# The second layer's modulation dot products move from the first model's stages into a merge stage

## The chip, the cores and the metric

One core of one Trainium2 chip runs the whole program in one launch. The metric is the device time of that launch in microseconds. TensorE (PE) multiplies matrices, VectorE (DVE) and ScalarE (ACT) work on vectors, SyncE (SP) issues the DMAs that bring data from HBM into on-chip memory. Each engine has its own instruction stream; they meet by semaphores.

## The reference

Two models run one after the other on one sequence of 256 tokens of width 1024, in float32. The first has two layers of attention and a mixture of experts. The second has two layers, and each of its layers is modulated by six vectors that depend on a condition `c` alone, not on the tokens:

```python
def decoder_layer(x, c, ..., w_ada, b_ada, ...):
    mod = jax.nn.silu(c.astype(F32)) @ w_ada + b_ada        # (1, 6 * 1024)
    shift1, scale1, gate1, shift2, scale2, gate2 = jnp.split(mod, 6, axis=-1)
    h = modulate(rms_norm_2(x, norm1_g), shift1, scale1)
    ...
    gates = jax.nn.sigmoid((h @ w_gate + b_gate).astype(F32))
    merged = jnp.zeros(x.shape, F32)
    for i, y in enumerate((y_ret, y_rwkv, y_conv)):
        merged = merged + gates[..., i * d:(i + 1) * d] * (y @ w_branch[i])
    x = x + gate1[:, None, :] * (merged @ w_o)
    h2 = modulate(rms_norm_2(x, norm2_g), shift2, scale2)
    ...
```

`w_ada` has 1024 x 6144 numbers a layer, 24 MB of float32. The product with the single row silu(c) is what is called the modulation's dot products here. `y_ret`, `y_rwkv` and `y_conv` come from `h` through retention, RWKV and a short convolution; behind the last line stand the experts, weighted with gate2.

## The kernel before

All weights stream from HBM in chunks of 2 MB (128 partitions x 4096 float32) through `ring`, six slots. `load(sp, n, ...)` puts chunk n into slot n % 6; from chunk 6 on SyncE first waits until TensorE has counted `w_used` up to n - 5, so chunk n is issued when chunk n - 6 has been used. SyncE works through its list in order: what stands behind a waiting load waits too.

The stages are blocks, one after another, and a block ends when all engines have ended their part. In the first model a layer has `project1` (the input projection, four chunks), `latents`, `turn_qk`, `attention`, `head_rms_out` (the output projection, two chunks) and `moe` (the experts). In the second model a layer has `project2` (chunks 0 to 10), several stages of retention and RWKV, then `merge` (chunks 11 to 19), `project_out2` (20, 21) and `moe` (from 22).

The modulation's dot products run on VectorE. A chunk of `w_ada` holds four blocks of 1024 columns; for each, one instruction multiplies it by silu(c) (`c_all`, the same row on all partitions) and accumulates the sum over the columns into one column of `mod_sums`. `ada_load` brings chunk i of a stage into one of two places of the `arena`; from the third on it waits for `ada_used`, that is, for the dots of chunk i - 2. `ada_dots` waits for its chunk and does its four dots. A layer of the second model needs 12 chunks, 48 dots. Before the change the first model's layer l does those of the second model's layer l: 8 chunks in `project1` (`ADA1`), placed three, three and two ahead of VectorE's copies of the projection out of PSUM, and 4 in `head_rms_out` (`ADA2`), ahead of the residual additions of j = 0, 1, 3 and 5. `project2` of the second model reads `mod_sums` at its start.

`merge` has 24 steps m = 8 i + d (branch i, output block d). TensorE computes the gate product (8 matmuls from `xnT`) and the branch product (4 matmuls) of a step into the two halves of bank m % 8; ScalarE applies the sigmoid; VectorE multiplies both (L1402, L1404), counts `taken`, and from step 8 on adds the result to `merged` (L1406). From step 8 on TensorE waits for `taken` of step m - 8. Each branch uses three ring chunks: one to its step 3 (gate), one to its step 7 (gate), one to the branch product of its step 7. Here chunk 17 to 25 are loaded: `for n in range(MERGE + RING, OUT2 + RING)`.

A matmul of float32 shows as two records in the trace, so a gate product is 16 records and a branch product 8.

Of the kernel before, what the change touches and what calls it, by code (L numbers as in the profile page):

```python
# [19 lines left out]
ALU = mybir.AluOpType  # L20
# [4 lines left out]
L = 2  # L25
# [85 lines left out]
SMALL1 = 2 * UQ_N + UKV_N + KT * R1_N  # L111
SMALL2 = 2 * MW + KT * R2_N
CONV, RWKV, LORA, RET, MERGE, OUT2, MOE2 = 0, 3, 6, 7, 11, 20, 22
ADA1, ADA2 = 8, 4
MOE1 = 6


def build(nc, dram, out):
    ctx = ExitStack()
    with ctx:  # L120
# [106 lines left out]
        def ada_sems():  # L227
            return [sem(f"ada_in{i}") for i in range(2)], sem("ada_used")

        def ada_load(sp, sems, l, i, places):  # L230

            ada_in, ada_used = sems
            if i >= 2:
                sp.wait_ge(ada_used, i - 1)
            sp.dma_start(ar(places[i % 2], SLOT), dram["w_ada2"][l, i]).then_inc(ada_in[i % 2], 16)

        def ada_dots(dve, sems, l, i, places):

            ada_in, ada_used = sems
            dve.wait_ge(ada_in[i % 2], 16 * (i // 2 + 1))  # L240
            for j in range(4):
                w = ar(places[i % 2] + D * j, D)
                last = nc.vector.scalar_tensor_tensor(w, w, 1.0, c_all, ALU.mult, ALU.mult,  # L243
                                                      accum_out=mod_sums[:, l, 4 * i + j:4 * i + j + 1])
            last.then_inc(ada_used, 1)

        def setup():
            in_loaded, x_loaded, c_loaded = sem("in_loaded"), sem("x_loaded"), sem("c_loaded")
# [137 lines left out]
        def project1(l, ada):  # L386
            scaled = sem("n1a_scaled")
            places = (4096, 8192)
            with nc.Block() as block:
                @block.sync  # L390
                def _(sp):
                    for i in range(ADA1):
                        ada_load(sp, ada, l, i, places)
                    if l == 0:
                        for n in range(4, 6):
                            load(sp, n, *first_chunks(1, 0)[n])
                    for n in range(MOE1, MOE1 + 4):
                        load(sp, n, moe1_chunk(l, n))
# [35 lines left out]
                @block.vector  # L434
                def _(dve):
                    dve.wait_ge(sets[turn[0]]["vec_in"], 48)
                    norm_scale(dve, scaled, V1("attn_norm"), xnT)
                    for b in (1, 3, 5, 7):
                        if b < 7:
                            for i in ((0, 1, 2), (3, 4, 5), (6, 7))[b // 2]:  # L440
                                ada_dots(dve, ada, l, i, places)
                        dve.wait_ge(w_used(), b // 2 + 1)
                        nc.vector.tensor_copy(dests[b], bank[b][:, 0:REST if b == 7 else 512])

# [257 lines left out]
        def head_rms_out(l, ada):  # L702
# [8 lines left out]
            with nc.Block() as block:  # L711
                @block.sync
                def _(sp):
                    for i in range(ADA1, ADA1 + ADA2):
                        ada_load(sp, ada, l, i, places)
                    for n in range(MOE1 + 4, MOE1 + 6):
                        load(sp, n, moe1_chunk(l, n))

# [31 lines left out]
                def _(dve):  # L750
# [6 lines left out]
                    for n in range(4, 6):  # L757
                        for i in range(4):
                            j = 4 * (n - 4) + i
                            if j in (0, 1, 3, 5):  # L760
                                ada_dots(dve, ada, l, ADA1 + (0, 1, 3, 5).index(j), places)
                            if i < 3:
                                dve.wait_ge(proj_ready, 3 * (n - 4) + i + 1)
                            else:
                                dve.wait_ge(w_used(), n + 1)
                            nc.vector.tensor_tensor(hT[:, j, :], hT[:, j, :], out_bank(j)[:, 0:T], ALU.add).then_inc(norms[0], 1)
# [581 lines left out]
        def merge(l):  # L1348

            pair_ready, gate_ready, taken, s_dve = sem("mrg_pair"), sem("mrg_gate"), sem("mrg_taken"), sem("mrg_dve")  # L1350
            ys = (y_ret, y_rwkv, y_conv)
            sg = ar(13824, 4, T)
            tmp = ar(0, 2, T)
            with nc.Block() as block:
                @block.sync
                def _(sp):
                    for n in range(MERGE + RING, OUT2 + RING):
                        load2(sp, l, n)

                @block.tensor  # L1360
                def _(pe):
# [19 lines left out]

                @block.scalar
                def _(act):
                    for i in range(3):
                        for d in range(KT):
                            m = KT * i + d
                            if d < KT - 1:
                                act.wait_ge(pair_ready, (KT - 1) * i + d + 1)
                            else:
                                act.wait_ge(w_used(), MERGE + 3 * i + 3)  # L1390
                            if m >= 4:
                                act.wait_ge(taken, m - 3)
                            nc.scalar.activation(sg[:, m % 4, :], bank[m % 8][:, 0:T], ACT.Sigmoid, bias=V2("b_gate_2")[:, m:m + 1]).then_inc(gate_ready, 1)

                @block.vector
                def _(dve):
                    then = step(dve, s_dve)
                    for m in range(3 * KT):
                        d = m % KT
                        dve.wait_ge(gate_ready, m + 1)  # L1400
                        if m < KT:
                            nc.vector.tensor_tensor(merged[:, d, :], sg[:, m % 4, :], bank[m % 8][:, T:2 * T], ALU.mult).then_inc(taken, 1)  # L1402
# [592 lines left out]
```

## Time and profile before

| | us |
|---|---|
| median of 3 timed runs | 2921.86 (2912.44 to 2928.99) |
| the profiled execution | 2913.63 |
| its span from first to last instruction | 2911.7 |
| TensorE busy | 2280.5 (78%) |
| VectorE busy | 737.8 (25%) |
| ScalarE busy | 369.1 (13%) |
| DMA | 778.84 MB, mean 267 GB/s |

The span is the time between the first and the last instruction of the profiled execution; the device time is some 2 us more. Busy shares are means over stages with different limits: the expert stages move 400 GB/s and more, other stages hardly any data. A row of the timeline has the start, the length, the engine, the line, the operation, output and inputs, the count, and in brackets how long the engine stood idle before it and what released it. "issue", "PEq" and the like stand for waits at the border of blocks.

### The profile page before, as it was taken

How to read it: one execution, taken by the hardware profiler on the slowest of the kernel's cores; microseconds unless marked ns; L12 is line 12 of the kernel's file. 1: busy time of each engine (PE TensorE's matmuls, PEld its weight loads, DVE VectorE, ACT ScalarE, POOL GpSimd, SP SyncE). 2: the span in 40 equal slices, each digit the busy share in tenths (PEclk: the TensorE clock that was granted, in tenths of full speed). 3: DMA queues.
4: the chain of work that ended last, by engine and by line, in shares of the span. 5: the costliest groups of instructions: out<-in, count | busy, mean ns of one | idle time of the engine just before them, and what ended most of it. 6: DMA issues, size and time to landing. Idle time of an engine off the chain costs nothing. (4 is left out here: it accounts for less than half of the span.)

```text
span 2911.7 us, 30995 instructions
## 1 busy us (share of the span) xinstructions
PE 2280.5 (78%) x12840; PEld 1430.8 (49%) x12841; DVE 737.8 (25%) x1659; ACT 369.1 (13%) x732; POOL 5.2 (0%) x16
## 2 busy tenths in 40 slices
PE   7788778788778987799867666689687998666765
PEld 5464335564336756678622122276476885222222
DVE  5661005561102145511200000012545112000001
ACT  1430000430001022010200000010311101000000
POOL 0000000000000000000000000000000000000000
PEclk9899889799889999789888887899896998878878
DMA  9549999247996420013499999964100335999997
GB/s 366 211 174 410 428 428 363 117 176 312 429 428 265 155 107 1 1 73 129 152 428 428 429 428 429 428 245 173 58 1 1 116 145 206 428 429 428 429 429 319
DMA packets 55688, 778.84 MB, mean 267 GB/s; under 512 B 6825, under 2 KB 7081, under 8 KB 7977
## 3 DMA queue, kind: packets, MB, share of 16 engines
q1 hardware_dynamic: 55592, 777.50, 64.4%
q8 instruction: 69, 1.13, 0.2%
q14 instruction: 27, 0.21, 0.0%
HBM read 776.42 MB, written 1.05 MB: 267 GB/s over the span
## 5 line engine op out<-in xcount | busy, mean ns | idle before, releaser
L1632 PE MATMUL bank<-ring,arena 128*32 128x512 f32 x3136 | 508.8, 786 | 329.1 <-DMA ring<-in_w_exp 325.3
L1632 PEld LDWEIGHTS bank<-ring,arena 128*32 128x32 f32 x3136 | 102.5, 127 | 726.6 <-DMA ring<-in_w_exp 488.1
L1657 PE MATMUL bank<-ring,arena 128*32 128x512 f32 x1568 | 197.7, 643 | 69.1 <-DMA ring<-in_w_exp 46.3
L850 PE MATMUL bank<-xnT,ring 128*128 128x256 f32 x960 | 212.1, 384 | 9.5 <-ACT xnT L366 9.5
L1812 DVE TENSOR_TENSOR arena<-bank,arena 128x256 f32<-128x256 f32 (+1 forms) x33 | 18.3, 554 | 791.0 <-PE bank L1632 561.5
L850 PEld LDWEIGHTS bank<-xnT,ring 128*128 128x128 f32 x960 | 185.2, 193 | 36.9 <-issue 11.2
L1372 PE MATMUL bank<-xnT,ring 128*128 128x256 f32 x768 | 177.0, 384 | 10.1 <-PEq L978 10.1
L1372 PEld LDWEIGHTS bank<-xnT,ring 128*128 128x128 f32 x768 | 148.1, 193 | 32.3 <-issue 11.7
L1602 PE MATMUL bank<-arena 128*128 128x256 f32 x592 | 142.0, 394 | 3.6 <-DVE arena L1823 3.6
L1602 PEld LDWEIGHTS bank<-arena 128*128 128x128 f32 x592 | 112.9, 196 | 63.3 <-issue 48.9
L1657 PEld LDWEIGHTS bank<-ring,arena 128*32 128x32 f32 x1568 | 50.5, 114 | 186.1 <-issue 96.8
L1594 PE MATMUL bank<-arena 128*128 128x128 f32 x1056 | 132.8, 288 | 3.4 <-DVE arena L1732 3.4
L1594 PEld LDWEIGHTS bank<-arena 128*128 128x128 f32 x1056 | 132.0, 204 | 5.4 <-DVE arena L1732 3.9
L243 DVE SCALAR_TENSOR_TENSOR arena<-arena 128x1024 f32<-128x1024 f32 x96 | 111.9, 1221 | 56.9 <-DMA arena<-in_w_ada 56.6
L1379 PE MATMUL bank<-arena,ring 128*128 128x256 f32 x384 | 90.7, 379 | 0.0
L1704 ACT ACTIVATE arena<-bank 128x256 f32<-128x256 f32 (+1 forms) x33 | 16.1, 487 | 562.0 <-PE bank L1632 562.0
L842 PE MATMUL bank<-ring,xnT 128*128 128x512 f32 x192 | 82.7, 592 | 0.0
L1823 DVE COPY arena<-bank 128x512 f32<-128x512 f32 x33 | 22.8, 692 | 228.5 <-PE bank L1657 228.5
L1379 PEld LDWEIGHTS bank<-arena,ring 128*128 128x128 f32 x384 | 73.0, 190 | 9.9
L1680 ACT COPY arena<-bank 128x512 f32<-128x512 f32 x33 | 19.3, 585 | 427.0 <-PE bank L1594 427.0
L856 DVE COPY arena<-bank 128x512 f32<-128x512 f32 x20 | 13.8, 691 | 226.3 <-PE bank L850 153.8
L1740 DVE COPY arena<-bank 128x512 f32<-128x512 f32 x33 | 22.8, 691 | 189.0 <-PE bank L1594 188.8
(322 smaller groups left out, 2414.9 us busy)
## 6 DMA issues: line engine op xcount, KB each, us to landing
ring<-in_w_exp SPq DMA_DIRECT2D x288, 2048.0 KB, 25.7
arena<-in_w_ada SPq DMA_DIRECT2D x24, 2048.0 KB, 8.0
ring<-in_w_in SPq DMA_DIRECT2D x20, 2048.0 KB, 20.2
ring<-in_w_merge SPq DMA_DIRECT2D x18, 2048.0 KB, 8.0
ring<-in_w_o SPq DMA_DIRECT2D x8, 2048.0 KB, 10.5
ring<-in_w_conv SPq DMA_DIRECT2D x6, 2048.0 KB, 26.2
ring<-in_w_rest SPq DMA_DIRECT2D x2, 1696.0 KB, 25.5
small<-in_small SPq DMA_DIRECT2D x2, 1440.0 KB
```

The lines of the kernel that those rows point to most:

```text
L243: last = nc.vector.scalar_tensor_tensor(w, w, 1.0, c_all, ALU.mult, ALU.mult, accum_out=mod_sums[:, l, 4 * i + j:4 * i + j + 1])
L842: last = nc.tensor.matmul(o[:, 0:MW], xnT[:, k, P * (not first):P * (not first) + P], w[:, k, :], start=k == 0, stop=k == KT - 1)
L850: last = nc.tensor.matmul(o[:, T * j:T * j + T], w[:, k, col:col + P], xnT[:, k, :], start=k == 0, stop=k == KT - 1)
L1372: last = nc.tensor.matmul(bank[m % 8][:, 0:T], w[:, k, P * (d % 4):P * (d % 4) + P], xnT[:, k, :], start=k == 0, stop=k == KT - 1)
L1379: last = nc.tensor.matmul(bank[m % 8][:, T:2 * T], w[:, k, P * d:P * d + P], ys[i][:, k, :], start=k == 0, stop=k == MT - 1)
L1594: last = nc.tensor.matmul(gather_banks[d // 4][:, P * (d % 4):P * (d % 4) + P], xtok[:, t, P * d:P * d + P], onehot[:, t, :], start=t == 0 ...
L1602: last = nc.tensor.matmul(bank[d // 2][:, T * (d % 2):T * (d % 2) + T], Yw[:, P * d:P * d + P], gwT, start=False, stop=ready is not None, ...
L1632: last = nc.tensor.matmul(o[rows(e), :], Xw[:, k, rows(e)], ring[:, slot(n), at:at + MW], start=k == 0, stop=k == KT - 1)
L1657: last = nc.tensor.matmul(o[rows(e), :], hidT[:, j, rows(e)], ring[:, slot(n), at:at + MW], start=j == 0, stop=j == ft - 1)
L1680: return nc.scalar.copy(Xw[:, 0:4, :], gather_banks[0][:, :].rearrange("p (d s) -> p d s", d=4)).then_inc(low_taken, 1)
L1740: return nc.vector.tensor_copy(Xw[:, 4:8, :], gather_banks[1][:, :].rearrange("p (d s) -> p d s", d=4)).then_inc(high_taken, 1)
L1823: nc.vector.tensor_copy(Yw[:, 0:MW], y0_bank[:, :]).then_inc(y0_taken, 1)
```

## The change

The first model's stages keep only the dots of the second model's layer 0: its 12 chunks are shared out over both layers of the first model, 4 in each `project1` and 2 in each `head_rms_out`. The 12 chunks of the second model's layer 1 go into `merge` of layer 0. There SyncE puts one `ada_load` ahead of each of the nine ring loads and three behind them; VectorE does two dots ahead of each step's multiplication, a chunk every two steps. `c_all` has been overwritten by then, so `c_row` is loaded again and silu(c) is made from a Sigmoid on ScalarE and a product on VectorE. The `merge` of layer 1 stays as it was.

```diff
--- before.py
+++ after.py
@@ -111,7 +111,7 @@
 SMALL1 = 2 * UQ_N + UKV_N + KT * R1_N
 SMALL2 = 2 * MW + KT * R2_N
 CONV, RWKV, LORA, RET, MERGE, OUT2, MOE2 = 0, 3, 6, 7, 11, 20, 22
-ADA1, ADA2 = 8, 4
+ADA_CHUNKS, ADA_P1, ADA_HEADS = 12, 4, 2
 MOE1 = 6
 
 
@@ -227,22 +227,24 @@
         def ada_sems():
             return [sem(f"ada_in{i}") for i in range(2)], sem("ada_used")
 
-        def ada_load(sp, sems, l, i, places):
+        def ada_load(sp, sems, l, ch, i, places):
 
             ada_in, ada_used = sems
             if i >= 2:
                 sp.wait_ge(ada_used, i - 1)
-            sp.dma_start(ar(places[i % 2], SLOT), dram["w_ada2"][l, i]).then_inc(ada_in[i % 2], 16)
-
-        def ada_dots(dve, sems, l, i, places):
+            sp.dma_start(ar(places[i % 2], SLOT), dram["w_ada2"][l, ch]).then_inc(ada_in[i % 2], 16)
+
+        def ada_dots(dve, sems, l, ch, i, places, c, js=range(4)):
 
             ada_in, ada_used = sems
-            dve.wait_ge(ada_in[i % 2], 16 * (i // 2 + 1))
-            for j in range(4):
+            if js[0] == 0:
+                dve.wait_ge(ada_in[i % 2], 16 * (i // 2 + 1))
+            for j in js:
                 w = ar(places[i % 2] + D * j, D)
-                last = nc.vector.scalar_tensor_tensor(w, w, 1.0, c_all, ALU.mult, ALU.mult,
-                                                      accum_out=mod_sums[:, l, 4 * i + j:4 * i + j + 1])
-            last.then_inc(ada_used, 1)
+                last = nc.vector.scalar_tensor_tensor(w, w, 1.0, c, ALU.mult, ALU.mult,
+                                                      accum_out=mod_sums[:, l, 4 * ch + j:4 * ch + j + 1])
+            if j == 3:
+                last.then_inc(ada_used, 1)
 
         def setup():
             in_loaded, x_loaded, c_loaded = sem("in_loaded"), sem("x_loaded"), sem("c_loaded")
@@ -389,8 +391,8 @@
             with nc.Block() as block:
                 @block.sync
                 def _(sp):
-                    for i in range(ADA1):
-                        ada_load(sp, ada, l, i, places)
+                    for i in range(ADA_P1):
+                        ada_load(sp, ada, 0, ADA_P1 * l + i, i, places)
                     if l == 0:
                         for n in range(4, 6):
                             load(sp, n, *first_chunks(1, 0)[n])
@@ -437,8 +439,8 @@
                     norm_scale(dve, scaled, V1("attn_norm"), xnT)
                     for b in (1, 3, 5, 7):
                         if b < 7:
-                            for i in ((0, 1, 2), (3, 4, 5), (6, 7))[b // 2]:
-                                ada_dots(dve, ada, l, i, places)
+                            for i in ((0, 1), (2,), (3,))[b // 2]:
+                                ada_dots(dve, ada, 0, ADA_P1 * l + i, i, places, c_all)
                         dve.wait_ge(w_used(), b // 2 + 1)
                         nc.vector.tensor_copy(dests[b], bank[b][:, 0:REST if b == 7 else 512])
 
@@ -711,8 +713,8 @@
             with nc.Block() as block:
                 @block.sync
                 def _(sp):
-                    for i in range(ADA1, ADA1 + ADA2):
-                        ada_load(sp, ada, l, i, places)
+                    for i in range(ADA_HEADS):
+                        ada_load(sp, ada, 0, L * ADA_P1 + ADA_HEADS * l + i, ADA_P1 + i, places)
                     for n in range(MOE1 + 4, MOE1 + 6):
                         load(sp, n, moe1_chunk(l, n))
 
@@ -757,8 +759,9 @@
                     for n in range(4, 6):
                         for i in range(4):
                             j = 4 * (n - 4) + i
-                            if j in (0, 1, 3, 5):
-                                ada_dots(dve, ada, l, ADA1 + (0, 1, 3, 5).index(j), places)
+                            if j in (1, 3):
+                                a = j // 2
+                                ada_dots(dve, ada, 0, L * ADA_P1 + ADA_HEADS * l + a, ADA_P1 + a, places, c_all)
                             if i < 3:
                                 dve.wait_ge(proj_ready, 3 * (n - 4) + i + 1)
                             else:
@@ -1349,13 +1352,24 @@
 
             pair_ready, gate_ready, taken, s_dve = sem("mrg_pair"), sem("mrg_gate"), sem("mrg_taken"), sem("mrg_dve")
             ys = (y_ret, y_rwkv, y_conv)
+            ada, c_in, c_ready = ada_sems(), sem("mrg_c"), sem("mrg_cready")
+            ahead = l + 1 < L
+            places, c_raw, c_now = (512, 4608), ar(8704, D), ar(9728, D)
             sg = ar(13824, 4, T)
             tmp = ar(0, 2, T)
             with nc.Block() as block:
                 @block.sync
                 def _(sp):
+                    if ahead:
+                        sp.dma_start(c_raw, dram["c_row"]).then_inc(c_in, 16)
                     for n in range(MERGE + RING, OUT2 + RING):
+                        if ahead:
+                            i = n - MERGE - RING
+                            ada_load(sp, ada, l + 1, i, i, places)
                         load2(sp, l, n)
+                    if ahead:
+                        for i in range(OUT2 - MERGE, ADA_CHUNKS):
+                            ada_load(sp, ada, l + 1, i, i, places)
 
                 @block.tensor
                 def _(pe):
@@ -1381,6 +1395,9 @@
 
                 @block.scalar
                 def _(act):
+                    if ahead:
+                        act.wait_ge(c_in, 16)
+                        nc.scalar.activation(c_now, c_raw, ACT.Sigmoid).then_inc(c_ready, 1)
                     for i in range(3):
                         for d in range(KT):
                             m = KT * i + d
@@ -1395,8 +1412,14 @@
                 @block.vector
                 def _(dve):
                     then = step(dve, s_dve)
+                    if ahead:
+                        dve.wait_ge(c_ready, 1)
+                        then(nc.vector.tensor_tensor(c_now, c_now, c_raw, ALU.mult))
                     for m in range(3 * KT):
                         d = m % KT
+                        if ahead:
+                            i = m // 2
+                            ada_dots(dve, ada, l + 1, i, i, places, c_now, range(2 * (m % 2), 2 * (m % 2) + 2))
                         dve.wait_ge(gate_ready, m + 1)
                         if m < KT:
                             nc.vector.tensor_tensor(merged[:, d, :], sg[:, m % 4, :], bank[m % 8][:, T:2 * T], ALU.mult).then_inc(taken, 1)
```

SyncE's list in `merge` of the second model's layer 0, before and then after. `in_w_ada` are the chunks with the dots' weights; the others are ring loads (chunk 17 first); a wait is printed under the first name that its semaphore had, so `e1_gwturned` is here `ada_used`.

```order
L199 DMA ring<-in_w_merge 128x4096 [waits w_used0] x3
L199 DMA ring<-in_w_o 128x4096 [waits w_used0] x2
L199 DMA ring<-in_w_exp 128x4096 [waits w_used0] x4
L1354 UNCONDITIONAL_BRANCH
```

```order
L1364 DMA arena<-in_c_row 128x1024
L235 DMA arena<-in_w_ada 128x4096
L199 DMA ring<-in_w_merge 128x4096 [waits w_used0]
L235 DMA arena<-in_w_ada 128x4096
L199 DMA ring<-in_w_merge 128x4096 [waits w_used0]
L235 DMA arena<-in_w_ada 128x4096 [waits e1_gwturned]
L199 DMA ring<-in_w_merge 128x4096 [waits w_used0]
L235 DMA arena<-in_w_ada 128x4096 [waits e1_gwturned]
L199 DMA ring<-in_w_o 128x4096 [waits w_used0]
...
L199 DMA ring<-in_w_exp 128x4096 [waits w_used0]
L235 DMA arena<-in_w_ada 128x4096 [waits e1_gwturned] x3
```

Nine ring loads stood alone; now each has a dot chunk ahead of it, and each dot chunk but the first stands behind a ring load that waits for TensorE.

VectorE's list at the same place, before and after, from the last step that only multiplies (step 7) on. L1402 and L1425, L1404 and L1427, L1406 and L1429 are the same operations in the two files, L244 is a dot; `e1_silu` is here `mrg_gate`, `e1_hid` `mrg_taken`, and `e1_hidT`, `e1_gw` the arrival of a dot chunk.

```order
L1402 TENSOR_TENSOR arena<-arena,bank 128x256 [waits e1_silu] x8
L1404 TENSOR_TENSOR arena<-arena,bank 128x256 [waits e1_silu]
L1406 TENSOR_TENSOR arena<-arena 128x256 [waits e1_hid]
L1404 TENSOR_TENSOR arena<-arena,bank 128x256 [waits e1_silu,e1_hidturned]
L1406 TENSOR_TENSOR arena<-arena 128x256 [waits e1_hid]
```

```order
L244 SCALAR_TENSOR_TENSOR arena,mod_sums<-arena 128x1024 x2
L1425 TENSOR_TENSOR arena<-arena,bank 128x256 [waits e1_silu]
L244 SCALAR_TENSOR_TENSOR arena,mod_sums<-arena 128x1024 [waits e1_hidT]
L244 SCALAR_TENSOR_TENSOR arena,mod_sums<-arena 128x1024
L1427 TENSOR_TENSOR arena<-arena,bank 128x256 [waits e1_silu]
L1429 TENSOR_TENSOR arena<-arena 128x256 [waits e1_hid]
L244 SCALAR_TENSOR_TENSOR arena,mod_sums<-arena 128x1024 [waits e1_hidturned]
L244 SCALAR_TENSOR_TENSOR arena,mod_sums<-arena 128x1024
L1427 TENSOR_TENSOR arena<-arena,bank 128x256 [waits e1_silu]
```

Each multiplication now has two dots ahead of it, and in every second step the first of them waits for a DMA.

VectorE's list in `project1` of layer 0, before and after (L443 and L445 are the copies out of PSUM):

```order
L443 COPY arena<-bank 128x512 [waits w_used0]
L243 SCALAR_TENSOR_TENSOR arena,mod_sums<-arena 128x1024 [waits ada_in0]
L243 SCALAR_TENSOR_TENSOR arena,mod_sums<-arena 128x1024 x3
L243 SCALAR_TENSOR_TENSOR arena,mod_sums<-arena 128x1024 [waits ada_in1]
L243 SCALAR_TENSOR_TENSOR arena,mod_sums<-arena 128x1024 x3
L443 COPY arena<-bank 128x512 [waits w_used0]
L443 COPY arena<-bank 128x424 [waits w_used0]
```

```order
L445 COPY arena<-bank 128x512 [waits w_used0]
L244 SCALAR_TENSOR_TENSOR arena,mod_sums<-arena 128x1024 [waits ada_in1]
L244 SCALAR_TENSOR_TENSOR arena,mod_sums<-arena 128x1024 x3
L445 COPY arena<-bank 128x512 [waits w_used0]
L445 COPY arena<-bank 128x424 [waits w_used0]
```

Four dots instead of eight stand between the last two groups of copies, and four instead of twelve in the group ahead of them.

## Rows read from the trace of the kernel before

**Rows 1.** Costliest groups: operation, count | busy us, mean ns | idle before, releaser

```profile
L243 DVE SCALAR_TENSOR_TENSOR arena<-arena 128x1024 f32<-128x1024 f32 x96 | 111.9, 1221 | 56.9 <-DMA arena<-in_w_ada 56.6
...
L1632 PE MATMUL bank<-ring,arena 128*32 128x512 f32 x3136 | 508.8, 786 | 329.1 <-DMA ring<-in_w_exp 325.3
```

**Rows 2.** Timeline, end of `project1` and start of `latents`, layer 0: start, length, what

```profile
72.86 5.25 PE L420 MATMUL bank<-ring,xnT 128*128 128x424 f32 x14
78.15 0.51 ACT L432 COPY arena<-bank 128x424 f32<-128x424 f32 x1 [11.82 <-PE bank L420]
86.09 1.19 DVE L443 COPY arena<-bank 128x512 f32<-128x512 f32 x2
87.57 0.42 ACT L471 ACTIVATE arena<-arena 128x256 f32<-128x256 f32 x1 [8.90 <-PEq L389]
92.64 1.54 PE L522 MATMUL bank<-cst,arena 128*128 128x128 f32 x6 [14.53 <-DVE arena L501]
```

**Rows 3.** Timeline, the same place in layer 1

```profile
497.29 5.25 PE L420 MATMUL bank<-ring,xnT 128*128 128x424 f32 x14
515.49 1.19 DVE L443 COPY arena<-bank 128x512 f32<-128x512 f32 x2
516.97 0.42 ACT L471 ACTIVATE arena<-arena 128x256 f32<-128x256 f32 x1 [13.88 <-PEq L389]
```

**Rows 4.** Timeline, last residual addition of `head_rms_out`, layer 0

```profile
193.11 0.42 DVE L766 TENSOR_TENSOR hT<-hT,bank 128x256 f32<-128x256 f32 x1 [1.81 <-PE bank L743]
```

**Rows 5.** Stretch, merge: length, busy PE, PEld, DVE, ACT, POOL, clock, DMA, GB/s

```profile
1259.40:1387.20 127.80, 126.18 (x576) 110.53 (x576) 16.90 (x40) 12.64 (x25) 0.00 (x0) 0.99 0.32 120
```

**Rows 6.** Timeline of the merge, layer 0: steps 0, 7, 15, last, next stage

```profile
1259.47 5.31 PE L1372 MATMUL bank<-xnT,ring 128*128 128x256 f32 x16 [5.03 <-PEq L978]
...
1297.43 3.62 PE L1372 MATMUL bank<-xnT,ring 128*128 128x256 f32 x16
...
1300.88 1.89 PE L1379 MATMUL bank<-arena,ring 128*128 128x256 f32 x8
...
1338.87 3.62 PE L1372 MATMUL bank<-xnT,ring 128*128 128x256 f32 x16
...
1386.72 0.42 DVE L1406 TENSOR_TENSOR arena<-arena 128x256 f32<-128x256 f32 x1
...
1387.69 15.74 PE L1428 MATMUL bank<-arena,ring 128*128 128x256 f32 x64 [2.04 <-PEq L1354]
```

**Rows 7.** Timeline of two dots, and landings of `w_ada` chunks in `project1`, layer 0

```profile
38.82 1.22 DVE L243 SCALAR_TENSOR_TENSOR arena<-arena 128x1024 f32<-128x1024 f32 x1
...
39.97 1.22 DVE L243 SCALAR_TENSOR_TENSOR arena<-arena 128x1024 f32<-128x1024 f32 x1
...
DMA to landing us min/median/max: 7.8/7.9/21.6
```

**Rows 8.** `w_merge` chunks issued in the merge: count, ns, first to last start

```profile
L199 SPq DMA_DIRECT2D ring<-in_w_merge x3: 328/328/328, 1280.4 to 1302.8; - x3
...
DMA to landing us min/median/max: 8.0/8.5/11.6
```

**Rows 9.** Clock: a timeline row, then stretches as in rows 5

```profile
22.42 29.55 PE L410 MATMUL bank<-xnT,ring 128*128 128x256 f32 x128 [3.42 <-DVE xnT L358]
...
92.60:100.60 8.00, 6.60 (x17) 4.06 (x18) 2.54 (x12) 2.31 (x6) 0.00 (x0) 0.61 1.01 430
...
540.00:556.00 16.00, 14.30 (x40) 9.31 (x38) 7.68 (x25) 4.74 (x14) 0.00 (x0) 0.58 0.00 1
112.00:128.00 16.00, 15.08 (x72) 10.31 (x73) 11.61 (x40) 7.41 (x23) 0.00 (x0) 1.00 0.00 1
1387.60:1395.60 8.00, 7.91 (x29) 6.71 (x30) 0.48 (x1) 1.28 (x1) 0.00 (x0) 0.79 0.99 421
```

**Rows 10.** Waits in the merge: who waited for whom, us in total, times, longest

```profile
DVE arena L1404 <- ACT arena L1393: 69.3, 16, 4.8
DVE arena L1402 <- ACT arena L1393: 41.2, 8, 7.9
```

## The prediction

> **What bounds the kernel now.** I read the page's costliest groups first, then the stretches, then the instructions in order of time at three places: the end of `project1` in each layer of the first model, the end of `head_rms_out`, and the merge of the second model's first layer. The groups show that the largest stages, the experts, wait for their weights: the first matmul of an item stood idle 329 us in all, 325 us of it for the DMA into `ring` [rows 1]. Such a stage starts with a full ring and then runs at the pace of the transfers, so it keeps its length; if what stands ahead of it ends earlier or later, it moves as a block. So I look for time only ahead of those stages.
>
> The dot products (96 instructions on VectorE) cost 112 us of busy time [rows 1]. Most lies beside matmuls, but not all. In `project1` of layer 0 TensorE ends at 72.86 + 5.25 = 78.1 and ScalarE's last copy at 78.15 + 0.51 = 78.7, while VectorE's last two copies, queued behind the dots, end at 86.09 + 1.19 = 87.3. The next block begins only then: ScalarE at 87.6 after 8.9 us idle, TensorE at 92.6 after 14.5 us [rows 2]. In layer 1 the same happens with more delay: TensorE ends at 497.29 + 5.25 = 502.5, VectorE at 515.49 + 1.19 = 516.7 [rows 3]. In `head_rms_out` the last residual addition waits 1.8 us for TensorE, not the other way round, so the dots there are already covered [rows 4].
>
> In the merge stage (128 us) TensorE is busy 126 us at a granted clock of 0.99, VectorE 17 us, and the DMA engines 0.32 of the time [rows 5]. TensorE's cadence is 5.18 us a step (from the start of step 7 to that of step 15 it takes 41.44 us): 3.45 for the gate product, 1.73 for the branch product [rows 6]. On paper the dots fit there twice over. Whether they fit depends on when their weights arrive.
>
> **The change, part by part.** A chunk is four dots. One dot takes 1.15 us from start to start [rows 7], so a chunk takes 4.6 us of VectorE. 12 of the 24 chunks leave the first model, six from each layer; 12 chunks, one transfer of `c_row`, one Sigmoid and one product of 1024 columns enter the merge of layer 0.
>
> *`project1`.* Two buffers make a chunk pair cost 4.6 us plus 7.9 us from issue to landing [rows 7], 12.5 us. Eight chunks end at 86 us, four of them therefore two pairs earlier, at 61, well before TensorE's 78.1. So the copies wait for TensorE alone and the block ends some 0.6 us after it, as ScalarE's does: 78.7 for 87.3 in layer 0, **-8.6 us**; 503.1 for 516.7 in layer 1, **-13.6 us** [rows 2, 3]. In `head_rms_out` two chunks less bring nothing. The head start of SyncE's loads of expert weights brings nothing either, as they land long before they are used.
>
> *Merge.* The order of SyncE decides. The queue holds dot chunk 0, ring load 17, dot chunk 1, load 18, dot chunk 2, and so on. Load 17+i waits for TensorE to free a ring slot; dot chunk i+1 stands behind it. The slots come free at steps 3, 7, 7, 11, 15, 15, 19, 23, 23, so dot chunks 1 to 9 are issued no earlier than that, while VectorE needs chunk i at step 2i, before it may do the multiplication that frees TensorE's bank. TensorE may be only eight steps ahead.
>
> A 2 MB load lands 8.0 us after its issue when alone; of the pair issued at the ends of step 7's two products, 1301.05 and 1302.77, the landings were 8.5 and 11.6 us after [rows 6, 8], that is 4.85 us apart. So a dot chunk issued right behind a ring load lands 8.0 + 4.85 = 12.85 us after that load's issue. Now the chain, in the times of the trace before:
>
> - Steps up to 15 run as before (VectorE is late, but less than eight steps). Load 21 is released at the end of step 15's gate product, 1338.87 + 3.62 = 1342.5 [rows 6]. Dot chunk 5 lands at 1355.3; two dots and step 10's multiplication (2.3 + 0.4) free step 18 at 1358.1. TensorE would have begun it at 1338.87 + 3 x 5.18 = 1354.4: a pause of 3.7 us.
> - After a pause of 3.4 us a run of 128 matmul records took 29.55 us [rows 9] against 27.6 at the cadence (5.18 us for 24 records), 1.9 us more, and after 5.0 us the merge's first 16 took 5.31 for 3.62, 1.7 us more [rows 6]. I add 1.7 us. Step 18 and the gate product of 19 end at 1358.1 + 3.45 + 1.7 + 1.73 + 3.45 = 1368.4.
> - Load 23 and dot chunk 7 follow: landing 1381.3, step 22 free at 1384.0 (second pause, 3.5 us), last gate product ends at 1384.0 + 10.3 = 1394.3.
> - Load 24, dot chunk 8, load 25, dot chunk 9 follow: landings of the dot chunks 1407.2 and 1416.9. TensorE has no work left. Steps 16 and 17 (2.3 + 0.9 + 2.3) end the dots of chunk 8 at 1412.7; chunk 9's end at 1422.4 and only then is chunk 11 issued; it lands 7.9 us later at 1430.3. Its two steps cost 2 x (2.3 + 0.9), end 1436.6.
> - The merge ends now at 1386.72 + 0.42 = 1387.1 [rows 6]: **+49.5 us**, of which some 7 on TensorE's side and 42 as a tail.
>
> The `c_row` load, Sigmoid and product stand at the start, where nobody waits for VectorE until step 8: nothing; uncovered they would cost a landing and two operations of a dot's width, about 8 + 2 x 1.2 us.
>
> *Clock behind the tail.* The output projection restarts after some 40 us of idle instead of 2.0. Its first 8 us now have a granted clock of 0.79; the first 8 us of `latents`, after 14.5 us idle, had 0.61 [rows 9]. At 0.55, between that and the lower level (1.2 GHz, 0.5), it loses 8 x (0.79 - 0.55) = **+1.9 us**.
>
> Sum: 49.5 + 1.9 - 8.6 - 13.6 = **+29.2 us**. The profiled execution took 2913.6 us, so 2942.8; the median of the three timed runs is 2921.9, and I forecast on that scale: 2951 us, 1.0% slower.
>
> The Trainium skill speaks against one term. "DMA: Bandwidth & Descriptors", section on the anatomy of one DMA, gives 2.0 us plus the bytes at 436 GB/s (fitted on the GpSimd path), which makes an estimate of 6.8 us for 2 MB; the rows here have 7.9 to 8.5, and I go by them. By the page the four landings that count in the chain would be some 1.1 us shorter each, the merge's term +45 and the sum +25.
>
> **The rivals.**
>
> 1. *Hidden after all* (0.06). VectorE waits 69.3 + 41.2 us in the merge, nearly 5 us in each of 24 steps [rows 10], and 48 dots need only 55 us; the 25 MB fit beside a DMA share of 0.32 too. If chunks arrived by the step that needs them, the merge would cost nothing and only the gain would stay: -22, 2900 us, faster. It becomes faster only if the merge grows by less than 20 us (22.2 less the clock term), under half of what the queue order gives. Against it: nothing lets SyncE pass a waiting ring load.
> 2. *Same sign, smaller* (0.12). In layer 1 the first 16 us of attention ran at a mean clock of 0.58, in layer 0 the same work at 1.00 [rows 9]: up to 16 x 0.42 = 6.7 us. If the shift removes that slow stretch, and the merge and what follows stand at their lower bound (no clock losses, landings of the shortest row, 7.8: 49.5 - 3.4 - 0.8 = 45.3), the sum is 45.3 - 22.2 - 6.7 = +16: 2938 us, and with the scatter of the runs it can look like no change.
> 3. *Slower still* (0.15). The slow stretch appears in layer 0 as well (+6.7), the merge's pauses cost twice what I took (+3.4), the four landings are 8.5 (+2.0) and the output projection's start is at 0.50 (2.3 for 1.9): 54.9 + 2.3 - 22.2 + 6.7 = +42: 2964 us.
> 4. *Forecast* (0.67): +20 to +40, 2941 to 2962 us.
>
> **How the numbers follow.** The range 2931 to 2967 holds the forecast and most of rivals 2 and 3; the three timed runs before lie between 2912 and 2929, so up to 8 us at either end is measurement. Half a per cent is 14.6 us, about what this measurement can tell from no change. Slower by more: the forecast, rival 3 and half of rival 2, 0.88. Within: the other half of rival 2 and a little of rival 1, 0.07. Faster: the rest of rival 1, 0.05.
>
> **What the profile would show.** Right: ScalarE's wait at the start of `latents` nearly gone (0.5 us for 8.9 and 13.9) and the block beginning at about 79; in the merge VectorE waiting for the DMA of the `w_ada` chunks from step 2 on, with two short pauses of TensorE (steps 18, 22), and about 40 us between the last branch product and the output projection. Wrong: no wait of VectorE for that DMA in the merge, or a merge under 150 us; a wait of the copies in `project1` that is still on the dots; or an expert stage whose length changes by more than its clock explains.

## The result, and the profile after

The changed kernel is slower: median 2946.0 us of 20 runs (2933.2 to 2961.1), before 2919.8 us of 20 (2907.1 to 2934.7); ratio 1.0084, interval 1.0067 to 1.0102. Of 2919.8 us that is +24.5 us (19.6 to 29.8). The profiled execution took 2948.5 us.

The page's costliest groups, which answer to [rows 1]:

```profile
L244 DVE SCALAR_TENSOR_TENSOR arena<-arena 128x1024 f32<-128x1024 f32 x96 | 112.8, 1222 | 135.6 <-DMA arena<-in_w_ada 135.3
```

The dots cost what they cost before (112.8 us busy). What stood idle ahead of them for their weights grew from 56.6 to 135.3 us.

The timeline at the end of `project1`, layer 0 and then layer 1, which answers to [rows 2, 3]:

```profile
74.95 5.25 PE L422 MATMUL bank<-ring,xnT 128*128 128x424 f32 x14
80.24 0.51 ACT L434 COPY arena<-bank 128x424 f32<-128x424 f32 x1 [11.82 <-PE bank L422]
80.24 0.60 DVE L445 COPY arena<-bank 128x424 f32<-128x424 f32 x1 [11.72 <-PE bank L422]
81.12 0.42 ACT L473 ACTIVATE arena<-arena 128x256 f32<-128x256 f32 x1 [0.37 <-PEq L391]
...
490.97 5.25 PE L422 MATMUL bank<-ring,xnT 128*128 128x424 f32 x14
496.26 0.60 DVE L445 COPY arena<-bank 128x424 f32<-128x424 f32 x1 [11.29 <-PE bank L422]
497.14 0.42 ACT L473 ACTIVATE arena<-arena 128x256 f32<-128x256 f32 x1 [0.37 <-PEq L391]
```

VectorE's last copy now waits for TensorE as ScalarE's does, and the next block begins 0.9 us behind TensorE's last product in both layers (before: 9.5 and 14.4 us).

The merge of layer 0 as a stretch, which answers to [rows 5] (same columns), and its waits, which answer to [rows 10]:

```profile
1246.00:1422.00 176.00, 128.54 (x576) 111.63 (x576) 72.78 (x137) 13.72 (x26) 0.00 (x0) 0.88 0.63 254
```

```profile
DVE arena L244 <- DMA arena<-in_w_ada: 97.8, 11, 20.0
...
PE bank L1386 <- DVE arena L1427: 6.8, 2, 3.5
```

128 us became 176 us. TensorE's work is the same, and it was held up only twice, for 6.8 us in all. VectorE waits 97.8 us for weights with the DMA engines busy 0.63 of the time: neither is at its limit. The timeline tells where these waits end. VectorE's dots that waited for a DMA, TensorE's pauses and the stage's end:

```profile
1279.71 1.23 DVE L244 SCALAR_TENSOR_TENSOR arena<-arena 128x1024 f32<-128x1024 f32 x1 [19.95 <-DMA arena<-in_w_ada]
...
1341.95 1.23 DVE L244 SCALAR_TENSOR_TENSOR arena<-arena 128x1024 f32<-128x1024 f32 x1 [12.29 <-DMA arena<-in_w_ada]
...
1344.72 5.41 PE L1386 MATMUL bank<-xnT,ring 128*128 128x256 f32 x16 [3.45 <-DVE arena L1427]
...
1367.96 1.22 DVE L244 SCALAR_TENSOR_TENSOR arena<-arena 128x1024 f32<-128x1024 f32 x1 [9.94 <-DMA arena<-in_w_ada]
...
1370.72 3.72 PE L1386 MATMUL bank<-xnT,ring 128*128 128x256 f32 x16 [3.33 <-DVE arena L1427]
...
1379.46 1.89 PE L1393 MATMUL bank<-arena,ring 128*128 128x256 f32 x8
...
1392.28 1.23 DVE L244 SCALAR_TENSOR_TENSOR arena<-arena 128x1024 f32<-128x1024 f32 x1 [17.94 <-DMA arena<-in_w_ada]
1402.04 1.23 DVE L244 SCALAR_TENSOR_TENSOR arena<-arena 128x1024 f32<-128x1024 f32 x1 [3.38 <-DMA arena<-in_w_ada]
...
1415.56 1.23 DVE L244 SCALAR_TENSOR_TENSOR arena<-arena 128x1024 f32<-128x1024 f32 x1 [0.73 <-DMA arena<-in_w_ada]
...
1421.51 0.43 DVE L1429 TENSOR_TENSOR arena<-arena 128x256 f32<-128x256 f32 x1
1422.49 16.32 PE L1451 MATMUL bank<-arena,ring 128*128 128x256 f32 x64 [41.14 <-PEq L1360]
```

SyncE's issues in the merge:

```profile
1379.66 0.33 SPq L199 DMA_DIRECT2D ring<-in_w_exp  x1
1380.03 0.43 SPq L235 DMA_DIRECT2D arena<-in_w_ada  x1
1381.38 0.33 SPq L199 DMA_DIRECT2D ring<-in_w_exp  x1
1381.75 26.23 SPq L235 DMA_DIRECT2D arena<-in_w_ada  x3
```

A dot chunk leaves 0.37 us behind the ring load that TensorE released, and its dots start 12 us later (1380.03 to 1392.28). TensorE ends its last product at 1381.35. Four more chunks are used after that, and the output projection starts 41 us later.

From stage to stage (each the time between the starts of the first products of two stages, after less before): `project1` of layer 0 -8.8 us, of layer 1 -13.5, merge +48.2, output projection +0.6, sum +26.5. The profiled execution is 34.9 us longer. Of what is left, 7.8 us lie in the attention of layer 1, which differs from run to run (experiment 9), and 2.4 at the program's start (its first projection product came 22.4 to 24.8 us into the span in the twelve profiles); the other stages together are 1.8 us shorter.

### The profile page after: what moved, and what is told of

Its sections match the earlier page's. It is cut to its first block and busy times, and to the rows that moved or that the text cites. A ratio compares the mean times of both kernels' runs of the same rounds, so it can differ in the third digit from the quotient of the medians.

```text
span 2946.7 us, 30991 instructions
## 1 busy us (share of the span) xinstructions
PE 2278.4 (77%) x12840; PEld 1437.4 (49%) x12841; DVE 738.7 (25%) x1660; ACT 370.4 (13%) x733; POOL 5.2 (0%) x16
## 5 line engine op out<-in xcount | busy, mean ns | idle before, releaser
L1655 PE MATMUL bank<-ring,arena 128*32 128x512 f32 x3136 | 502.3, 777 | 341.8 <-DMA ring<-in_w_exp 337.6
L1680 PE MATMUL bank<-ring,arena 128*32 128x512 f32 x1568 | 188.8, 619 | 69.2 <-DMA ring<-in_w_exp 46.5
L244 DVE SCALAR_TENSOR_TENSOR arena<-arena 128x1024 f32<-128x1024 f32 x96 | 112.8, 1222 | 135.6 <-DMA arena<-in_w_ada 135.3
L1451 PE MATMUL bank<-arena,ring 128*128 128x256 f32 x256 | 60.0, 398 | 43.2 <-PEq L1360 43.2
L1393 PE MATMUL bank<-arena,ring 128*128 128x256 f32 x384 | 90.7, 379 | 0.0
L1846 DVE COPY arena<-bank 128x512 f32<-128x512 f32 x33 | 22.8, 692 | 219.6 <-PE bank L1680 219.6
L1393 PEld LDWEIGHTS bank<-arena,ring 128*128 128x128 f32 x384 | 73.0, 190 | 9.9
L1451 PEld LDWEIGHTS bank<-arena,ring 128*128 128x128 f32 x256 | 51.2, 201 | 51.7 <-issue 43.9
```

The costliest lines, as they stand in the source:

```text
L244: last = nc.vector.scalar_tensor_tensor(w, w, 1.0, c, ALU.mult, ALU.mult, accum_out=mod_sums[:, l, 4 * ch + j:4 * ch + j + 1])
L1393: last = nc.tensor.matmul(bank[m % 8][:, T:2 * T], w[:, k, P * d:P * d + P], ys[i][:, k, :], start=k == 0, stop=k == MT - 1)
L1451: last = nc.tensor.matmul(out_bank(4 * (n - OUT2) + j)[:, 0:T], w[:, k, P * j:P * j + P], merged[:, k, :], start=k == 0, stop=k == KT - 1)
L1655: last = nc.tensor.matmul(o[rows(e), :], Xw[:, k, rows(e)], ring[:, slot(n), at:at + MW], start=k == 0, stop=k == KT - 1)
L1680: last = nc.tensor.matmul(o[rows(e), :], hidT[:, j, rows(e)], ring[:, slot(n), at:at + MW], start=j == 0, stop=j == ft - 1)
L1846: nc.vector.tensor_copy(Yw[:, 0:MW], y0_bank[:, :]).then_inc(y0_taken, 1)
```

## The experiments

All ratios are to the kernel before, run beside them on the same chip. Experiments 1 to 4 ran on one chip, 5 to 8 on a second, 9 and 10 on a third, so medians are compared across these groups only by their ratios. "Merge" is the time from the merge's first gate product to the first output projection product; before has 128.2 us, the changed kernel 176.4.

**1. The same transfers in another order.** The dot chunks stand in SyncE's list where they are needed: three ahead of ring load 17, five ahead of 18, and so on, all twelve ahead of load 23.

```diff
-                    for n in range(MERGE + RING, OUT2 + RING):
-                        if ahead:
-                            i = n - MERGE - RING
-                            ada_load(sp, ada, l + 1, i, i, places)
+                    i = 0
+                    for n, due in zip(range(MERGE + RING, OUT2 + RING), (3, 5, 5, 7, 9, 9, 12, 12, 12)):
+                        while ahead and i < due:
+                            ada_load(sp, ada, l + 1, i, i, places)
+                            i += 1
                         load2(sp, l, n)
```

> The changed kernel with nothing but SyncE's order in the merge altered: each dot chunk is issued ahead of the first ring load that is released later than the place is free (chunks 0 to 2, load 17, chunks 3 and 4, loads 18 and 19, chunks 5 and 6, load 20, chunks 7 and 8, loads 21 and 22, chunks 9 to 11, loads 23 to 25). Same instructions, same bytes. Theory (the queue order makes the dot chunks late): the merge goes back to 128 to 131 us from 176, TensorE has no pause and no tail, and the kernel is 22 us faster than before, about 2898 us. Rival A (VectorE's dots ahead of the multiplications cost the time, 55 us of work): the merge stays near 176, 2946 us. Rival B (the bytes of the dot chunks crowd out the ring loads): the merge stays above 160, since the bytes are the same.

Measured: median 2894.9 us, ratio 0.9905 (0.9867 to 0.9942); merge 128.3 us. Its stretch and its waits:

```profile
1245.50:1373.30 127.80, 126.31 (x576) 110.54 (x576) 74.08 (x137) 13.67 (x26) 0.00 (x0) 0.99 0.81 321
```

```profile
DVE arena L244 <- DMA arena<-in_w_ada: 12.1, 3, 5.0
```

The same bytes and the same dots now lie wholly beside TensorE's 126 us, at a DMA share of 0.81. All +48 us came from the order of the queue, and what is left is the gain of `project1`, with 1.7 us more in the output projection (33.8 us for 35.5 before): the kernel is faster than both.

**2. The merge's part alone.** The first model as before (8 and 4 chunks a layer), and the changed merge on top; the sums are made twice.

```diff
-                    for i in range(ADA_P1):
-                        ada_load(sp, ada, 0, ADA_P1 * l + i, i, places)
+                    for i in range(8):
+                        ada_load(sp, ada, l, i, i, places)
```

> The first model as before the change (all 24 chunks there), and the changed merge on top, which computes the second layer's 48 sums a second time. Only the merge's part of the change is on trial. Theory: the merge takes 176 us, the rest is as before, +48 to +50 us on the kernel before: about 2969 us. Rival C (the cost sits elsewhere than in the merge, or the first model's gain is smaller than 22 us): a difference to before that is well under 48.

Measured: 2965.2 us, ratio 1.0155 (1.0110 to 1.0200), that is +45.3 us (32 to 58); merge 176.4 us, within 0.1 us as long as in the changed kernel. The two parts add up.

**3. Half of the dots, all transfers.** As 2, but only two of the four dots of each chunk in the merge.

```diff
-                            ada_dots(dve, ada, l + 1, i, i, places, c_now, range(2 * (m % 2), 2 * (m % 2) + 2))
+                            ada_dots(dve, ada, l + 1, i, i, places, c_now, (3 * (m % 2),))
```

> As the run with the merge added to the kernel before, but in the merge only two of a chunk's four dots are made (the first and the last; the sums are there already from the first model). Transfers, waits and their order stay. Theory (arrival decides): the arrivals hardly move, the merge is 168 to 170 us, +40 to +42 on before, about 2961 us. Rival A (the time of the dots): half of the cost goes, +24, about 2944 us.

Measured: 2957.0 us, ratio 1.0121 (1.0073 to 1.0170); merge 171.2 us, +43.0, a little above the 168 to 170 that I expected. Halving VectorE's added work took off 5 of 48 us. Were the work the cost, it would have been half.

**4. All dots, no transfers.** As 2, but the 48 dots of the merge read what stands in the two places already and write to a scrap tile. It leaves out the twelve transfers and with them the second set of sums.

```diff
-                        if ahead:
-                            i = n - MERGE - RING
-                            ada_load(sp, ada, l + 1, i, i, places)
...
+                                last = nc.vector.scalar_tensor_tensor(w, w, 1.0, c_now, ALU.mult, ALU.mult, accum_out=scrap[:, 4 * i + j:4 * i + j + 1])
```

> The first model as before the change, and in the merge all 48 dots on whatever lies in the two places, their sums into an unused tile, without transfers of dot chunks and without waits for them (left out: those 12 transfers; the layer's sums come from the first model). Theory: VectorE has room, the merge stays at 128 to 131 us, the kernel is as before, 2920 to 2923 us. Rival A: the merge stays near 176 us and the kernel at about 2968.

Measured: 2922.1 us, ratio 0.9991 (0.9966 to 1.0015); merge 128.2 us. In its waits VectorE waits for ScalarE as it did before, only shorter (30.8 us against 69.3 [rows 10]):

```profile
DVE arena L1426 <- ACT arena L1405: 30.8, 16, 2.4
```

48 dots, a transfer of `c_row`, the Sigmoid and its product cost nothing in this stage. With 3 this clears VectorE's work.

**5 and 6. The dot chunks one and two ring loads earlier.** The edit of 1 with `(2, 3, ..., 10)` and `(3, 4, ..., 11)`.

> The changed kernel with each dot chunk moved one ring load up in SyncE's list of the merge (chunks 0 and 1, load 17, chunk 2, load 18, and so on). Theory (each chunk is as late as the ring load ahead of it): chunk i now follows load 15+i instead of 16+i, the chain of landings starts one release earlier and the tail shrinks, but doesn't go. By the chain of the prediction with this order the merge takes about 160 us, 16 less than as changed: kernel about +10 on before, 2930 us. A rival by which the order matters only as a whole (all or nothing) gives 176 or 128.

> The same with two ring loads of lead (chunks 0 to 2, load 17, chunk 3, load 18, and so on). Theory: the merge takes about 154 us, because the last chunks then wait for the two places instead of the loads; kernel about +4 on before, 2925 us.

Measured: merge 160.2 and 154.0 us; medians 2928.3 and 2922.5, ratios 1.0044 (1.0016 to 1.0071) and 1.0035 (1.0007 to 1.0062). TensorE's restart behind the merge, of 5 and then of 6:

```profile
1403.07 3.32 PE L1452 MATMUL bank<-arena,ring 128*128 128x256 f32 x7 [33.89 <-PEq L1360]
```

```profile
1398.19 4.18 PE L1452 MATMUL bank<-arena,ring 128*128 128x256 f32 x11 [27.67 <-PEq L1360]
```

One chunk of lead takes a round of "release, transfer, dots" off the tail, the second less. The chain with which I had forecast the merge gave these two lengths too. Moving every chunk by a fixed distance isn't enough: the ring's slots come free unevenly, singly and in pairs, and the chunks are needed evenly.

**7. Another queue.** SyncE keeps only its ring loads. ScalarE issues the dot chunks: two at the start, chunk m/2 + 1 behind the sigmoid of each even step m.

```diff
+                            if ahead and m % 2 == 0 and 2 <= m < 2 * ADA_CHUNKS - 2:
+                                ada_load(act, ada, l + 1, m // 2 + 1, m // 2 + 1, places)
```

> The changed kernel with the merge's dot chunks issued by ScalarE (two at the start, then chunk i behind the sigmoid of step 2i-2), while SyncE keeps the ring loads alone. Theory: no dot chunk can stand behind a ring load, so the merge is 128 to 134 us and the kernel about 22 us faster than before, 2899 us, as with the order by due time. If two queues that transfer at the same time slowed each other, or ScalarE's issues delayed the sigmoids, the merge would be over 140.

Measured: 2893.7 us, ratio 0.9916 (0.9882 to 0.9951); merge 128.3 us. A dot chunk that need not stand behind a ring load costs nothing, by order or by queue.

**8. Six chunks in each `project1`, none in `head_rms_out`** (on top of 1). I had read from [rows 3, 4] that six would be hidden there.

```diff
-                            for i in ((0, 1), (2,), (3,))[b // 2]:
+                            for i in ((0, 1, 2), (3, 4), (5,))[b // 2]:
```

> The order by due time in the merge, and the second model's first 12 chunks in the first model's input projections alone, six each, none in its output projections. Six chunks end three pairs after the first arrival, about 74 us into layer 0, before TensorE's last product at 78 to 80. Theory: project1 ends as with four chunks, so the kernel is as with the order by due time, about 2897 us. Rival (any dot in project1 costs in proportion): half of the 22 us comes back, about 2908.

Measured: 2892.1 us, ratio 0.9934 (0.9903 to 0.9964), not told apart from 1. In layer 0 the block ended with TensorE, as with four chunks. In layer 1 it did not (timeline):

```profile
510.08 1.23 DVE L244 SCALAR_TENSOR_TENSOR arena<-arena 128x1024 f32<-128x1024 f32 x1 [1.86 <-DMA arena<-in_w_ada]
511.81 0.51 ACT L434 COPY arena<-bank 128x424 f32<-128x424 f32 x1 [11.82 <-PE bank L422]
514.67 1.19 DVE L445 COPY arena<-bank 128x512 f32<-128x512 f32 x2
516.14 0.42 ACT L473 ACTIVATE arena<-arena 128x256 f32<-128x256 f32 x1 [3.82 <-PEq L391]
```

The last chunk came at 510.08, its dots and the two copies behind them ended 3.5 us after ScalarE's copy, and ScalarE waited 3.82 us instead of 0.37. So six are hidden in layer 0 only.

**9. Products that nobody reads, at the start of attention** (on top of 1). The segments that differ from run to run asked for a reason. The attention's part of a layer (from its first product to `head_rms_out`'s) took 46.7 us or, in eleven of the twenty stretches of the ten profiles up to here, between 52.8 and 60.6, though these kernels do the same there. (The expectation below says nine; counted again it is eleven.) Clock and records of two such stretches of the changed kernel, layer 1 and layer 0:

```profile
522.00:538.00 16.00, 15.90 (x40) 10.29 (x41) 6.89 (x24) 4.11 (x14) 0.00 (x0) 0.52 0.01 1
106.00:122.00 16.00, 15.48 (x73) 10.48 (x73) 11.86 (x42) 7.46 (x24) 0.00 (x0) 1.00 0.00 1
```

The granted clock is at 1.2 GHz in the one and 2.4 GHz in the other. In the slow one the lower level began 0.5 us behind the attention's first product and lasted 30.7 us (from 522.6 to 553.3); over the eleven slow stretches it began 0.4 to 1.0 us behind that product and lasted 13.7 to 30.7:

```profile
508.90:522.50 13.60, 10.37 (x51) 6.59 (x49) 6.01 (x14) 7.56 (x17) 0.00 (x0) 1.00 0.00 0
522.60:553.20 30.60, 30.60 (x80) 19.58 (x81) 12.62 (x43) 7.09 (x26) 0.00 (x0) 0.50 0.00 1
```

In both stretches TensorE stood 1.70 us just before, waiting for VectorE (timeline, layer 1 and layer 0):

```profile
522.10 0.49 PE L607 MATMUL bank<-arena 64*128 64x128 f32 x2 [1.70 <-DVE arena L646]
...
106.52 0.48 PE L607 MATMUL bank<-arena 64*128 64x128 f32 x2 [1.70 <-DVE arena L646]
```

The edit fills that pause with three products of constants into a bank that is overwritten later:

```diff
+                    for _ in range(3):
+                        nc.tensor.matmul(bank[0][:, 0:P + T], K("ones"), K("causal"), start=True, stop=True)
```

> The order by due time in the merge, and three unused products (128x384, into a bank that the attention overwrites) at the start of TensorE's part of the attention, where it waits 1.7 us for VectorE. In the ten profiles so far the way from the attention's first product to the next stage took 46.7 us with a full granted clock, or 52.8 to 60.6 with a slow stretch, in nine of twenty cases. Theory (the pause of 1.7 us right after a block border lets the clock fall): with the pause filled both layers take 46.7 us, and the median falls by some 5 to 10 us below the order by due time, to about 2887 us. Rival (the slow stretch comes from what TensorE did before, or from the thinness of the attention's own products): it still appears, and the median stays at about 2895.

Measured: 2884.7 us (2884.2 to 2886.8 in six runs), ratio 0.9888 (0.9853 to 0.9922). The same place:

```profile
102.96 2.17 PE L631 MATMUL bank<-cst 128*128 128x384 f32 x6 [1.02 <-PEq L543]
105.06 0.48 PE L607 MATMUL bank<-arena 64*128 64x128 f32 x2
```

From the first product that counts, both attention stretches took 46.7 us. The products nobody reads are not free: with 1.02 us of idle time and 2.1 of filler for a pause of 1.70, the way from `turn_qk` to `head_rms_out` is 53.5 us, 1.4 more than in a short stretch without them (52.1) and less than in any slow one. The six runs lie within 2.6 us; the kernel before, beside them on the same chip, lay within 28, and the runs of 1 within 23.

That 9 is faster than 1 at the median is not shown: the intervals of their ratios overlap. And two of the ten runs of 7, without filler, took 2878.2 and 2878.3 us, less than any run of 9 (though on another chip). What 9 shows is the missing scatter and the two short stretches. That it was the filled pause, and not the later start or the added work of TensorE, is argued: no run put the same products elsewhere or only delayed the attention.

**10. The same at the start of `latents`** (on top of 9): eight such products while ScalarE and VectorE make the norm.

> As the run with the filler in the attention, and eight unused products (5.2 us) at the start of TensorE's part of latents as well, where it waits 4.7 to 6.0 us. Theory: the clock stays at its upper level there too, the product behind it (16 records of 128x384) takes 5.1 us for 7.0 to 8.0, so 2 to 3 us less in each layer: about 5 us below the run with one filler, 2882 us. Rival: the filler makes no difference to that product, or delays it.

Measured: 2882.2 us (2880.5 to 2882.9 in six runs), ratio 0.9876 (0.9842 to 0.9911), the lowest median of all versions; its slowest run is faster than the fastest of 9. The products behind the norm:

```profile
85.78 5.43 PE L533 MATMUL bank<-small,arena 128*128 128x384 f32 x16 [1.47 <-DVE arena L512]
```

and in 9, which had none before them there:

```profile
86.15 7.15 PE L531 MATMUL bank<-small,arena 128*128 128x384 f32 x16 [1.36 <-DVE arena L512]
```

From the first product behind the norm to the next stage it took 12.7 and 12.6 us in the two layers, for 15.0 and 15.9 in 9. But the eight products took 5.4 us and held that first product up, by 0.2 us in layer 0 and 1.5 in layer 1, so the stage as a whole is 2.2 and 1.9 us shorter. I had expected 5 us off the median; it fell by 2.5, and where the rest of those 4 us went is open.

## Why the prediction was right, and where its sizes were off

- **`project1`**: -8.6 and -13.6 forecast, -8.8 and -13.5 measured. ScalarE's wait is 0.37 us, I had said 0.5. That both agree to 0.2 us is in part luck: in the profiles of kernels with the same chunks there, the stage's length varied from 60.0 to 63.0 us (layer 0, four chunks), 58.7 to 61.3 (layer 1, four), 70.2 to 71.6 and 73.9 to 78.9 (eight).
- **Merge**: +49.5 forecast, +48.2 measured. In the times of after (all 13.4 us earlier) my chain had the arrivals of chunks 5, 7, 8, 9 and 11 at 1341.9, 1367.9, 1393.8, 1403.5 and 1416.9, and the dots start at 1341.95, 1367.96, 1392.28, 1402.04 and 1415.56. It rests on landings read from the trace. The Trainium skill's "DMA: Bandwidth & Descriptors", section on the anatomy of one DMA, from whose fit for the GpSimd path I had estimated 6.8 us for a lone 2 MB load and +45 for the merge, is not borne out for these loads by SyncE: the shortest landing of a dot chunk in this merge is 7.8 us, and +48.2 lies nearer to the rows' sum.
- **The pauses**: two of 3.7 and 3.5 us forecast, 3.45 and 3.33 measured. The restart after the first took 5.41 us for 3.62, 1.8 us more, where I had added 1.7; after the second it took 3.72, where I had added 1.7 again. That second 1.7 is the term that was too large: chunks 8 and 9 came 1.5 us earlier than in my chain, and of this 1.3 us was left at the merge's end. The Trainium skill's "TensorE: Matmul & The Clock Gate", section "HAM oscillation — how this bites in real kernels", describes a loop that waits some 3 to 5 us for a DMA in each round and restarts cold every time. Here, where TensorE waited for VectorE, the first pause, of 3.45 us, was followed by such a restart, and the second, of 3.33 us, was not.
- **Clock behind the tail**: +1.9 forecast, +0.6 measured. The first 8 us of the output projection have a granted clock of 0.71, I had taken 0.55; before it was 0.79 [rows 9]. That makes 8 x (0.79 - 0.71) = 0.6 us, though the idle time ahead was 41 us for 2. Nor is 0.79 what 2 us of idle time always leave: in experiment 1 the output projection began after 1.98 us at a granted clock of 1.00 and took 33.8 us for 35.5.

```profile
1422.40:1430.40 8.00, 7.91 (x26) 6.61 (x27) 0.48 (x1) 1.28 (x1) 0.00 (x0) 0.71 0.01 3
```

- **What I had costed at nothing**: the dots themselves, `c_row`, Sigmoid and product cost nothing (experiment 4). `head_rms_out` kept its length (38.3 us in both kernels), and so did the expert stages within 1 us; they moved as blocks.
- **The sum** of the terms was +29.2 forecast and +26.5 measured; the ratio gives +24.5 (19.6 to 29.8).
- **The rivals.** "Hidden after all" fell by the queue order, as argued: experiments 1 and 7 show that the very same work is hidden once no dot chunk stands behind a waiting ring load. The slow attention stretch of rivals 2 and 3 did neither vanish nor appear because of the change: it comes and goes between kernels alike there, and neither layer of experiment 9 has it. I had priced it at up to 6.7 us; it cost 6 to 14.
- **A claim that failed**: that six chunks in `project1` would be hidden in both layers. Experiment 8 shows 3.5 us of them in layer 1.

Open stays why one and the same pause of 1.70 us is followed once by 2.4 and once by 1.2 GHz. One thing sorts all twenty stretches: how long ago the granted clock had risen to 2.4 GHz, in `latents`, when the attention's first product began. It was 12.65 to 13.25 us in the eleven slow stretches and 13.30 to 14.16 us in the nine short ones (in the changed kernel 13.20 in layer 1 and 14.04 in layer 0). A shift of tenths of a us ahead of the attention went with 6 to 14 us in it; what makes it so, no run tells. The experiments show only that with the products in the pause both profiled stretches were short, and that no run's time left room for a long one.

## What to carry to other kernels

In a queue that issues in order, a transfer inherits every wait ahead of it: place each one by when it can be issued and when it is needed, not one for one between others, or give it a queue of its own. Free time on the engine and free DMA bandwidth in a stage say only that the work could fit; follow slot release, issue, landing and use for each chunk before you count it as hidden. And where runs of one kernel scatter by a per cent, look for a short pause of TensorE ahead of a stretch whose clock differs from run to run.

## What the runs showed of the hardware

- A pause of 1.70 us of TensorE could be followed, within 1 us of the restart, by 13.7 to 30.7 us at a granted clock of 0.5 (11 of 20 stretches), or by 1.00 throughout. The slow form cost 6 to 14 us per layer (52.8 to 60.6 us for 46.7). With three products of 2.17 us in all placed in the pause it appeared in neither layer of the two profiles, at a price of 1.4 us per layer, and the runs of each kernel lay within 2.6 us.
- Two pauses of almost the same length (3.45 and 3.33 us), 26 us apart in the same loop, were followed by a slow product (5.41 us) and by one at nearly full speed (3.72 us).
- After some 2 us of idle time the first 8 us of the same products had a granted clock of 0.79 in one kernel and 1.00 in another; after 41 us of idle time, 0.71.
